# A hybrid decoder on one core: block 1's attention and last value product moved behind block 0's output product

## What is computed

```python
def stick_breaking(q, k, v):         # 8 heads of 64
    z = einsum('bhqd,bhkd->bhqk', q, k) * dh ** -0.5
    mask = key_pos[None, :] < q_pos[:, None]
    log_stay = where(mask, log_sigmoid(-z), 0.0)
    suffix = cumsum(log_stay, axis=3, reverse=True) - log_stay
    a = where(mask, exp(log_sigmoid(z) + suffix), 0.0)
    return einsum('bhqk,bhkd->bhqd', a, v)
...
def layer_ab(h, w_in, w_alpha2, b_alpha2, gla_norm, w_out):
    q_sb, k_sb, v_sb, q_g, k_g, v_g, g_g, a_lr = split(h @ w_in)
    o_sb = stick_breaking(q_sb, k_sb, v_sb)
    o_g = gla(q_g, k_g, v_g, log_a)      # gated linear attention, 4 heads, chunks of 64 tokens with a carried state
    o_g = rmsnorm(o_g) * gla_norm * silu(g_g)
    return concatenate([o_sb, o_g]) @ w_out
...
def peer(h, w_q, subkeys, u_tab, v_tab):   # 8 heads, 128 experts a token
    q = h @ w_q
    scores = q . subkeys                   # two sets of 128 keys a head
    idx, gate = top 16 of the pair sums of the top 16 of each set
    act = gelu(u_tab[idx] . h)
    return sum(gate * act * v_tab[idx])
```

## Time and profile before

| | us |
|---|---|
| median of 3 runs | 1674.19 (1673.43 to 1676.97) |
| the profiled execution | 1672.77 |
| its span | 1671.0 |
| PE busy | 1440.7 (86%) |
| VectorE, ScalarE, GpSimd busy | 983.1, 681.5, 658.7 |
| gathers, x512, GpSimd | 648.8, first at 181.58 |
| L1363, the gather products | 983.2 |
| bytes moved | 637.54 MB, of which gathers 536.90 MB |

### The profile page before, as it was taken

One profiled execution on the slowest core, in us unless ns is written; L12 is line 12 of the kernel. 1 busy time (PEld: TensorE's weight loads), 2 busy tenths in 40 slices (PEclk: granted clock), 3 DMA queues, 4 the chain that ended last, 5 costly groups with the idle time before them and its releaser, 6 DMA issues.

```text
span 1671.0 us, 14524 instructions
## 1 busy us (share of the span) xinstructions
PE 1440.7 (86%) x4326; PEld 705.8 (42%) x4326; DVE 983.1 (59%) x2484; ACT 681.5 (41%) x1854; POOL 658.7 (39%) x537
## 2 busy tenths in 40 slices
PE   6999799998777988998888897989888897897786
PEld 5665466653222333443334444444334343342222
DVE  1132666776778755643446755664554785777654
ACT  1672334453345534333334433533334452544433
POOL 1000244464464433344244342424333553445673
PEclk9999799999899999999999999999999998999999
DMA  5323799999999999999999999999999999999996
GB/s 205 112 101 113 294 369 421 412 422 423 421 422 421 423 421 423 420 423 423 421 421 422 391 422 421 398 401 394 422 422 422 421 420 424 421 421 421 421 421 263
DMA packets 82190, 637.54 MB, mean 382 GB/s; under 512 B 9264, under 2 KB 9408, under 8 KB 10560
## 3 DMA queue, kind: packets, MB, share of 16 engines
q0 software_dynamic: 73728, 536.90, 77.8%
q1 hardware_dynamic: 8064, 98.65, 14.3%
q10 hardware_dynamic: 320, 1.07, 0.2%
HBM read 635.53 MB, written 1.05 MB: 381 GB/s over the span
## 4 chain that ended last, share of the span: by engine, by line
PE 41%; DMA 38%; DVE 8%; ACT 5%; issue 5%; POOL 4%; DVEq 0%; POOLq 0%; ACTq 0%
DMA ring<-in_peer_uv,experts 35%; PE acc L1363 22%; PE work L1149 7%; PE work L1164 6%; DVE ring L1043 4%; POOL ring L543 4%; PE work L1139 2%; PE acc L1328 1%; DMA weights<-in_c_w_in 1%; ACT diag L721 1%; ACT gelus L719 1%; DMA weights<-in_peer_w_q 1%; PE work L1347 1%; DMA x<-in_x 1%; ACT gelus L718 1%
## 5 line engine op out<-in xcount | busy, mean ns | idle before, releaser
L1363 PE MATMUL acc<-ring,diag 128*128 128x512 f32 x2048 | 983.2, 616 | 181.1 <-ACT diag L721 179.6
L543 POOL DMA_INDIRECT ring<-in_peer_uv,experts x512 | 648.8, 1267 | 872.7 <-PE acc L1363 721.7
L1043 DVE CUSTOM_DVE_ANT_0 ring<-ring,h 128x1024 f32<-128x1024 f32 x512 | 625.5, 1226 | 466.8 <-DMA ring<-in_peer_uv,experts 458.2
L1363 PEld LDWEIGHTS acc<-ring,diag 128*128 128x128 f32 x2048 | 373.8, 194 | 717.7 <-ACT diag L721 371.3
L718 ACT ACTIVATE gelus<-dots 128x1 f32<-128x1 f32 x512 | 103.0, 201 | 681.9 <-DVE dots L1043 681.0
L721 ACT ACTIVATE diag<-ident,gelus 128x128 f32<-128x128 f32 x512 | 205.6, 401 | 16.7
L1149 PE MATMUL work<-weights,hT 128*128 128x512 f32 x352 | 168.5, 611 | 12.0 <-DMA weights<-in_c_w_in 12.0
L719 ACT ACTIVATE gelus<-gelus,gates 128x1 f32<-128x1 f32 x512 | 150.8, 295 | 16.6
L1164 PEld LDWEIGHTS work<-hT,weights 128*128 128x128 f32 x896 | 109.8, 194 | 28.1 <-issue 26.4
L1164 PE MATMUL work<-hT,weights 128*128 128x128 f32 x896 | 109.9, 277 | 0.9 <-DMA weights<-in_peer_w_q 0.9
L1149 PEld LDWEIGHTS work<-weights,hT 128*128 128x128 f32 x352 | 68.2, 198 | 93.3 <-issue 80.1
(11 more groups left out here) (173 smaller groups left out, 749.1 us busy)
## 6 DMA issues: line engine op xcount, KB each, us to landing
weights<-in_c_w_in SPq DMA_DIRECT2D x16, 2048.0 KB, 11.9
weights<-in_peer_w_q SPq DMA_DIRECT2D x11, 2048.0 KB, 11.5
weights<-in_c_w_out SPq DMA_DIRECT2D x8, 2048.0 KB, 11.8
weights<-in_ab_w_in SPq DMA_DIRECT2D x6, 2048.0 KB, 8.3
ring<-in_peer_uv,experts POOLq DMA_INDIRECT x512, 14.8
weights<-in_ab_w_out SPq DMA_DIRECT2D x2, 2048.0 KB, 7.8
keysT<-in_peer_keys SPq DMA_DIRECT2D x2, 1024.0 KB, 9.5
z<-in_peer_w_q SPq DMA_DIRECT2D x1, 2048.0 KB, 7.8
```

The lines of the kernel that those rows point to most:

```text
L543: pool.indirect_dma_start(ring[:, step % SLOTS, :], None, uv_rows, bass.IndirectOffsetOnAxis(ap=experts[:, b, step:step + 1], axis=0))\
L1043: nc.vector.tensor_tensor_reduce(out=ring[:, k, 0:D], in0=ring[:, k, 0:D], in1=h[:, b, :], scale=1.0, scalar=0.0, op0=ALU.mult, op1=ALU.ad ...
L1363: last = nc.tensor.matmul(acc[2 * b + n][:, :], diag[:, k, :], ring[:, k, D + n * CH:D + (n + 1) * CH], start=False, stop=True, skip_group ...
```

## The change

The stage `MIX0` is taken apart into stages of `PLAN`, and the attention is batched otherwise. Scores now go into the four `acc` banks, in six batches of four 128 x 128 blocks: batches 0 and 1 are block 0's eight heads, batches 2 to 5 are block 1's, two heads each with both key blocks. The suffix sums are added onto the scores in the same bank (no second score product), the mask too. In front of block 0's output product now stand: batches 0 and 1, the projections, the gate product of both blocks, the value product of block 0 only (`GV 0`), block 0's head outputs (`SOUT 0`), the first two state sums, block 0's readout.

Behind it stand: scores of batches 2 and 3, `GV 1` (its weight is a separate DMA of two halves into `scores1` and `v_norm`, in place of a chunk), the third state sum, scores of batches 4 and 5, block 1's readout. Behind the ranking of head 0 the batches' log part, sums and exponents (`LOG`, `STICKE` 2 to 5) and block 1's gated norm (`GLAOUT 1`). Block 1's head outputs, its output product, residual, norm and transposes, and the ranking of head 1 are laid behind the first 13 gather steps; the query projections of the following steps are placed anew.

GpSimd's first gather waits for the scores of all six batches, its fifth for the transposes of block 1's gated output. x is loaded on SP's queue ahead of the first weights. The ffn gains are loaded with the keys; the spatial weights (0.5 MB), whose tile now holds the values, come behind `SOUT 1`. The weight chunks of the second and third query products still wait for the last quarters of the output product (`out_full` 3 and 4), which now lie behind gather steps 3 and 4.

```diff
 PLAN = ([("COLS",)] + normed_now("mix0", 0, 1) + transposed("mix0", 0, 1)
-        + [("PROJQK",), ("SPATIAL",), ("STICK0",), ("PROJV",), ("QKEYS", 0), ("MIX0",),
-           ("OUT", 0, 0, 0), ("GLAREAD",), ("OUT", 0, 1, 0), ("GLAOUT", 0), ("OUT", 0, 0, 1), ("GLAOUT", 1), ("OUT", 0, 1, 1),
-           ("OADD", 0), *normed_now("ffn0", 0),
-           ("OUT", 1, 0, 0), ("TRANSPOSE", (0,), "ffn0"), ("HTAKE", (0,), "ffn0")]
-        + scored(0, 0, 0, (0,)) + [("DTAKE", 0, 0, 0, (0,)), ("OUT", 1, 0, 1)]
-        + scored(0, 0, 0, (1,))
-        + [("OUT", 1, 1, 0), ("OUT", 1, 1, 1)] + ranked_now(0, 0, 0)
-        + [("DTAKE", 0, 0, 0, (1,)), ("OADD", 1), *normed_now("ffn0", 1)]
-        + transposed("ffn0", 1) + ranked_now(0, 0, 1)
+        + [("PROJQK",), ("STICKZ", 0), ("STICKZ", 1), ("SOFT", 0), ("LOG", 0), ("SOFT", 1), ("LOG", 1), ("PROJV",),
+           ("RANK",), ("QKEYS", 0), ("STICKE", 0), ("ALPHA",), ("STICKE", 1), ("GQ",), ("GK",), ("GG", 0), ("KD",),
+           ("GG", 1), ("GS",), ("GV", 0), ("WOUT",), ("SOUT", 0), ("KV", 0),
+           ("OUT", 0, 0, 0), ("GLAREAD", 0), ("OUT", 0, 1, 0), ("GLAOUT", 0), ("STICKZ", 2), ("STICKZ", 3),
+           ("OUT", 0, 0, 1), ("OUT", 0, 1, 1), ("OADD", 0), *normed_now("ffn0", 0), ("GV", 1),
+           ("TRANSPOSE", (0,), "ffn0"), ("HTAKE", (0,), "ffn0")]
+        + scored(0, 0, 0, (0,))[:-1] + [("KV", 1), ("QDOT", 0, 0, 0, (0,)), ("DTAKE", 0, 0, 0, (0,)),
+           ("STICKZ", 4), ("STICKZ", 5), ("GLAREAD", 1), ("SOFT", 2, 3, 4, 5)]
+        + scored(0, 0, 0, (1,)) + ranked_now(0, 0, 0)
+        + [("LOG", 2, 3, 4, 5), ("DTAKE", 0, 0, 0, (1,)), ("STICKE", 2), ("STICKE", 3), ("STICKE", 4), ("STICKE", 5),
+           ("GLAOUT", 1)]
...
 def parts_of_layer0():
+    out = [(0, ("SOUT", 1)), (6, ("SPATIAL",)), (20, ("CAUSAL",)), (1, ("OUT", 1, 0, 0)), (2, ("OUT", 1, 1, 0)), (3, ("OUT", 1, 0, 1)), (4, ("OUT", 1, 1, 1))]
+    out += ranked(0, 0, 0, 1) + [(7, ("OADD", 1))] + normed(7, "ffn0", 1)
+    out += [(10, ("TRANSPOSE", (1,), "ffn0")), (12, ("HTAKE", (1,), "ffn0"))]
...
                     for step in range(i0, i1):
                         t = first_step(layer, b) + step
                         pool.wait_ge(experts_ready, 1 + IDS_ORDER[layer, b, step // TOPK])
+                        if t == 0:
+                            pool.wait_ge(scores_full, BATCHES)
+                        elif t == SLOTS // 2:
+                            n = BANKS["GLAOUT", 1]
+                            pool.wait_ge(full[n % WB], n // WB + 1)
...
+            def stick_soft(batches):
+                for i in batches:
+                    act.wait_ge(scores_full, i + 1)
+                    last = nc.scalar.activation(stick[i], acc[STICK_BANK[i]][:, :], ACT.Abs)
+                link(last)
+                for i in batches:
+                    last = nc.scalar.activation(stick[i], stick[i], ACT.Exp, scale=-1.0)
+                link(last)
+                for i in batches:
+                    nc.scalar.activation(stick[i], stick[i], ACT.Ln, bias=1.0).then_inc(soft_ready, 1)
...
+            def stick_sums(i):
+                pe.wait_ge(log_ready, i + 1)
+                w, s = acc[STICK_BANK[i]], stick[i]
+                last = nc.tensor.matmul(w[:, :], suffix[:, 0, :], s, start=False, stop=True, skip_group_check=True)
...
```

More of the change, by code:

```diff
@@ L28 @@
 WB = 4
[L33 to L51 removed]
+BATCHES = 6
 N_CONSTS = 2
[L53 removed]
+N_MASKS = 14
 IDENT_MASKS = 2
@@ L307, in trunk @@
         first_chunk = z[:, :].rearrange("p (k n) -> p k n", n=CH)
-        suffix = slots(9)[:, 768:768 + 2 * P].rearrange("p (a b) -> p a b", a=2)
+        suffix = stick_masks[:, 0:2, :]
+        before = stick_masks[:, 2, :]
+        beyond = stick_masks[:, 3, :]
         gain_cols = consts[:, MIX_COLS:MIX_COLS + 2 * KT]
@@ L857, in gla_gated, with gla_carry @@
                 last.then_inc(gla_in, 1)
-            def gla_carry(n0):
-                for c in range(3):
-                    n = n0 + c
+            def gla_carry(n0, chunks):
+                for n, c in enumerate(chunks, n0):
                     w = await_bank(dve, n)
@@ L1230, in gla_keys, with gla_sums @@
                     last.then_inc(full[(n0 + k) % WB], 1)
-            def gla_sums(n0, values):
-                for c in range(3):
-                    own_copies(values[c // 2], 1)
-                    w = claim_bank(pe, n0 + c)
+            def gla_sums(n0, chunks):
+                for n, c in enumerate(chunks, n0):
+                    w = claim_bank(pe, n)
                     for j in range(2):
                         last = nc.tensor.matmul(w[:, j * T:(j + 1) * T], kd[:, c, j, :],
-                                                v_g[:, c // 2, j * T:(j + 1) * T], start=True, stop=True)
-                    last.then_inc(full[(n0 + c) % WB], 1)
+                                                v_g[c // 2][:, j * T:(j + 1) * T], start=True, stop=True)
+                    last.then_inc(full[n % WB], 1)
             def gla_scores(n0):
@@ new lines, in gla_out @@
+            def gla_out(n, b):
+                pe.wait_ge(gla_states, 2 if b == 0 else 3)
+                pe.wait_ge(scores_masked, 2 * (b + 1))
+                w = claim_bank(pe, n)
+                for hd in range(GH):
+                    cols = slice(hd * GDV, (hd + 1) * GDV)
+                    nc.tensor.matmul(w[:, cols], scT[:, b, hd, :], v_g[b][:, cols], start=True, stop=True)
+                    for c in (2 * b, 2 * b + 1):
+                        if c:
+                            at = c % 2 * GC
+                            last = nc.tensor.matmul(w[at:at + GC, cols], qz[:, hd, c * GC:(c + 1) * GC],
+                                                    state[:, c - 1, hd // 2, :], start=False, stop=True,
+                                                    skip_group_check=True)
+                last.then_inc(full[n % WB], 1)
@@ new lines, in stick_score @@
+            def stick_score(i):
+                if i == 4:
+                    pe.wait_ge(x_ready, 1)
+                w = acc[STICK_BANK[i]]
+                for k, (hd, kb, qb) in enumerate(in_batch(i)):
+                    last = nc.tensor.matmul(w[:, k * P:(k + 1) * P], kz[:, hd, kb * P:(kb + 1) * P],
+                                            qT[:, hd // 2, qb * P:(qb + 1) * P],
+                                            start=(k == 0), stop=True, skip_group_check=True)
+                last.then_inc(scores_full, 1)
@@ new lines, in stick_out @@
+            def stick_out(n, b):
+                pe.wait_ge(prob_ready, BATCHES if b else 2)
+                w = claim_bank(pe, n)
+                for j in range(4):
+                    for r in range(2):
+                        hd = 2 * j + r
+                        rows, cols = slice(64 * r, 64 * r + 64), slice(hd * SBD, (hd + 1) * SBD)
+                        for kb in range(b + 1):
+                            prob = prob1[:, hd, kb, :] if b else prob0[:, hd, :]
+                            last = nc.tensor.matmul(w[rows, j * P:(j + 1) * P], v_sb[:, kb, cols], prob,
+                                                    start=(kb == 0), stop=(kb == b))
+                last.then_inc(full[n % WB], 1)
```

476 lines of the change are left out of this document (225 added, 251 removed).

## The result

The changed kernel takes **1657.56 us** (median of 4 runs, 1655.07 to 1659.40) against 1674.49 for the kernel before on the same chip: ratio 0.9895, 95% interval 0.9882 to 0.9908. A second measurement, beside the experiments, gave 1654.06 (0.9883, 0.9868 to 0.9898). The profiled execution took 1655.07, its span is 1653.2 us, 17.8 less than before.

What follows compares the result with a forecast made beforehand. Behind the first expert rows the full DMA queue was taken to bound the kernel, in front of them TensorE. Earlier starts less queue holes put the 35.4 MB mark 16.3 us earlier, off 1672.8 profiled: median 1658, range 1649 to 1668.

Steps and rivals of the forecast that it cites:

- Step 1: Kernel start: x loaded in front of the weights lets the query and key products start at 14.1, 5.6 us earlier.
- Step 2: Mixers up to the first output product: batching and moved work take out 26.2 us, first output product at 106.6.
- Step 3: First output product to first gather: 33.7 us to the key product at 140.3, first gather at 151.0 instead of 181.58.
- Step 4: In front of the fifth gather: block 1's transposes, partly at half clock, leave the queue empty for 9.0 us.
- Step 5: First eight gather steps: output products run the queue dry for 2.1, 2.7 and 0.9 us; full from 199.7.
- Step 6: Cross-check by TensorE's work through the gather steps: step 43 stands at 303.9, 17.1 us earlier.
- Rival C: Gather steps 8 to 45: TensorE becomes the bound and the queue can run dry again; -8 to -10, 1665; chance 0.14.
- Rival B: Around the fifth gather and step 0: clock stays full or comes back at once; -23, 1651; chance 0.17.
- E: First gather steps: half clock stays through the pile; 1682 if through step 15; chance 0.07 together with F.
- F: Fifth gather: block 1's chain holds it until block 0's lead is spent, transposes at 186; chance 0.07 together with E.
- D: Kernel start: x gains nothing because the weights queue behind it; -11, 1663; chance 0.08.

Runs made afterwards that it cites:

- bef_x: Kernel before with only the two loads of x moved in front of the weights on SP's queue: 1669.28 us, ratio 0.9962.
- after2: Second measurement of the changed kernel itself, with no edit: 1654.06 us, ratio 0.9883 to the kernel before.
- gv_front: Changed kernel with block 1's value product put back in front of block 0's output product: 1660.79 us, ratio 0.9916.
- best_warm: Kernel best plus four products that nobody reads, one before batch 2's sums, three before block 1's readout transposes: 1649.90 us, ratio 0.9853.
- gla_early: Changed kernel with block 1's gated output ahead of batches 2 to 5's log part and sums, accumulator start waiting for the exponents: 1655.23 us, 0.9885.
- hold0: Changed kernel with the first gather, too, waiting for block 1's gated output, so rows 0 to 3 don't move early: 1662.61 us, 0.9923.
- thin: Changed kernel leaving out three of every four products of block 1's output product (values then not the reference's): 1655.38 us, 0.9874.
- sout_early: Changed kernel with block 1's head outputs moved from behind step 0 to before block 1's gated output: 1651.37 us, 0.9864.
- reord: Changed kernel taking both halves of the first column half of block 1's output product first: 1654.50 us, 0.9879.
- best: Changed kernel with the edits of gla_early, sout_early and reord together: 1650.84 us, ratio 0.9856.

## Why the prediction was right, and where its sum was not

The forecast was 1658, the measurement 1657.56 and 1654.06. That the first is within half a microsecond is luck: the two measurements of one kernel lie 3.5 us apart, and the terms of steps 4 and 5 were too dear and partly made up for by others. The mechanism, less unused queue time in front and an unchanged rest, is what the runs show: 16.3 us were foretold for the profiled execution, 17.8 and 20.3 were measured in the two.

**Step 1, x.** 14.1 foretold, 14.37 measured; shown by bef_x. x's second half was in by 5.80, where the estimate that the prediction makes with the figures of the Trainium skill, DMA: Bandwidth & Descriptors, section Anatomy of one DMA, said 5.2; that section gives them for loads issued by GpSimd, and these were issued by SP.

**Step 2, the mixers.** First output product at 106.6 foretold, 108.14 measured, and 106.33 in after2. From the start of the projections to there it is 91.95 us in after2 (92.5 foretold). The 1.5 us between are no part of the change: in the changed kernel's profiled execution the query and key products of both blocks (128 records) took 29.70 us instead of 27.88. The terms of this step (batching 14.0, value product 6.87, waits 2.6 and the rest) were right in their sum; no run shows them one by one.

**Step 3.** Key product done at 140.3 foretold, 141.65 measured; first gather 151.0 foretold, 152.60 (150.79 in after2). gv_front shows the cover that this step counts on (a wait of 3.90 us without it).

**Step 4, the gap: size and meaning wrong.** The fifth gather was foretold for 170.0 and went out at 168.79. The reason stood (the transposes), the clock was half right: after the first wait the first sum ran at half clock, but the clock came back within the sums (1.02 us from 159.05 on), fell again in the wait of 5.08 us for the norm, and so met transposes and accumulator start. Step 0, for which 3.8 us were foretold, took 1.89; step 1 took 3.41 instead. (The Trainium skill, TensorE: Matmul & The Clock Gate, section The HAM clock gate, has the throttled state as the default and activity as what releases it; these rows agree, and best_warm, which added activity, does too.) The queue did not stand empty for 9.0 us: 283 and 39 GB/s are 2.6 + 3.6 = 6.2, since the four rows kept it busy until about 165.5 (foretold 163.0) and the fifth left 1.2 us sooner. And gla_early shows that closing it gains nothing measurable, because the pile behind it then empties the queue. The sum added gap and pile, which is right for this one order of work; what the prediction did not see is that the two are exchanged for one another when one is closed.

**Step 5, the pile.** Holes of 5.7 us foretold, 1.0 + 0.9 + 2.7 = 4.6 measured (371, 383 and 310 GB/s); the queue was full from 200. Together with step 4 the sum was 3.9 us too dear, the slow start took 1.8 of them: 18.8 us less unused time where 16.3 stood, and 17.8 less span. In after2, where step 1 met the full clock, the holes are 1.6 us (401, 403 and 390 GB/s) and the unused time is 23.3 us less: in that execution the sum was 7 us too dear.

**Step 6, TensorE's ledger.** 17.1 earlier foretold at step 43; the row that it lets go leaves at 304.55, before at 323.75 (19.2 earlier):

```profile
323.75 1.56 POOL L543 DMA_INDIRECT ring<-in_peer_uv,experts  x1 [1.21 <-PE acc L1363]
```

**The rivals.** Rival C: from 210 to 320 TensorE was busy for all 110 us and the queue full at 420 GB/s, so it did not bind there; it binds in the pile and in short stretches near 1000 us, before as after. Rival B, a clock that stays full, comes nearest to best_warm, but there the gap is closed too: the clock is worth 3.1 us at the pile's end, and too little to measure in the median; its 7 us in the changed kernel were not tested. E: the clock was back at 1.00 in 190 to 200 (0.53 from 180 to 182 was the last half speed in the pile). F: block 1's transposes stood at 166.90 and not at 186, and the earlier start of the first four rows is worth 6.3 us of queue (hold0). D fell with bef_x.

## What to carry to other kernels

Count queue time that goes unused up to the point from which the queue is full, in bytes, and not gap by gap: a hole in front of a pile of TensorE work and the holes within that pile are one debt, and filling one opens the other. What paid here is TensorE work moved out of the chain in front of step 1 and laid where TensorE waits for another engine (2.0 us of work and 1.5 us of wait, 2.7 us gained in the median). That 10 us left out behind step 1 (thin) are worth less than that is not shown; that they are not worth 10 is (0.9856, the lower end of thin's interval, is 6.5 us under the changed kernel's 0.9895). A single execution of this kernel says little below 5 us: the spans apart from the unused time differ by that much, so time several, and take the profile for places and reasons.

## What the runs showed of the hardware

**The start of TensorE is a lottery that the clock column doesn't show.** The 128 records of the query and key products take 27.88 us in six profiled executions (before, bef_x, after2, sout_early, reord, best_warm) and 29.70 to 30.15 in the eight others, whatever the edit, the same kernel among them (changed and after2). Windows of the changed kernel, then of after2:

```profile
14.00:18.00 4.00, 3.63 (x9) 2.94 (x10) 0.00 (x0) 0.00 (x0) 0.00 (x0) 1.00 0.38 156
```

```profile
14.00:18.00 4.00, 3.62 (x17) 3.24 (x18) 0.00 (x0) 0.00 (x0) 0.00 (x0) 1.00 0.34 135
```

9 records in the time of 17, with the granted clock given as 1.00 in both. What decides it was not found; both kinds occur on each chip of the experiments.

**Four products in waiting time kept the clock up** in best_warm: 1.10 us for the first batch's sum instead of 2.05, and a granted clock of 1.00 over 140 to 170 where best has 0.83. Whether three in front of the transposes and one in front of the sums are all needed was not tried.
